# Mixers whose transposed input is split block by block, loads issued from another queue, and transposes moved into products: one change to a thirteen-stage fp32 kernel

## The chip, the cores and the metric

The kernel runs on one core of one Trainium2 chip. The metric is the device time of one execution, in microseconds (us). TensorE is PE in the profile, VectorE is DVE, ScalarE is ACT, GpSimd is POOL, SyncE is SP. A few more names of the profile: PSUM banks hold PE's results (128 partitions x 512 fp32), SBUF holds everything else.

## The reference

Two blocks of two layers each run over x, 256 tokens by 1024 features, batch 1, all in fp32. The thirteen stages in order are ffn, hgrn, ffn, ffn, fox, ffn, ffn, conv, ffn, kv, ffn, nsa, ffn. Cut to what is needed here:

```python
def rmsnorm(x, g): return x * rsqrt(mean(x * x) + EPS) * g
def swiglu(h, w_in, w_out):                 # every ffn stage: x += 0.5 * swiglu(rmsnorm(x))
    gate, up = split(h @ w_in, 2)           # w_in 1024 x 5632
    return (silu(gate) * up) @ w_out        # w_out 2816 x 1024
# hgrn: q, z, i, g = h @ w_in (1024 x 4096); gated linear recurrence; rmsnorm(o) * silu(g) @ w_out
# fox:  q, k, v, g, z_f = h @ w_in (1024 x 4112); attention with forgetting; (o * sigmoid(g)) @ w_out
# conv: b, c, v = h @ w_in (1024 x 3072); causal convolution of width 3 over c * v; (b * y) @ w_out
# kv:   rmsnorm(h, kv_norm) @ w_kv (1024 x 1536); two of its six parts are compressed by a small
#       MLP (w1, gelu, w2) over windows of 32 tokens with position vectors added; it is not added to x
# nsa:  q, gates = h @ w_q; three attentions over the results of kv (compressed, selected, window),
#       with a table of relative biases; mixed by sigmoid gates; @ w_o
```

## The kernel before, in words

**Numbers in two parts.** Every fp32 operand of a large product is split into a high part, rounded to PE's shorter fp32r form, and a low part, the rest. A product is three matmuls per piece k of 128 of the contraction: high times high and the two mixed ones (`pe_product`; lines 385 to 387 feature-major, 128x256, lines 390 to 392 token-major, 128x512). The 256 tokens are two tiles t of 128; the 1024 features are eight pieces k (KT). A feature-major result spans both tiles, so its product needs both tiles' operands from the first matmul on; a token-major one needs one tile.

**Who does what.** SP streams the weights (`raw_in`, `raw_out`). ACT writes each high part (`w_hi`, line 404), DVE each low part (`w_lo`, line 414), and PE multiplies. Products are chunks of 512 columns, numbered through the whole program; while PE is in chunk n, ACT and DVE split chunk n+1. Results alternate between two banks, `bank[0]` and `bank[1]`; four more, `accs`, accumulate over a stage; two, `tr`, take transposes. Each engine's order is fixed by the order of the Python code. Semaphores carry every wait. There is no scheduler.

**Slots.** Within a chunk's product, PE calls a slot function before piece k of tile t; in chunks with slots ACT and DVE call their own slot function in the same place between the parts of their splits (`elementwise_chunk`, by_tile). The slots hold the small work of the mixers: the recurrence's steps in hgrn (`hg_slots`), scores and values in fox (`fx_slots`), the relative biases in ffn 5, the compression in ffn 6 (`pe_compress_slot`, `act_compress_slot`). (ffn 5 and ffn 6 are the sixth and seventh ffn counted from 0, ahead of and behind kv.)

**A stage's start.** x is kept token-major (`x_tok`) and must be transposed and normed. In the mixers PE multiplies x by `diag_`, the identity scaled by 1/rms of each token, so one matmul turns and norms a block (`pe_turn_x`, line 473). The norm is a chain over ACT (squares, line 483; root, line 490) and DVE (lines 521, 523, then `diag_`, line 532). DVE then multiplies by the gain into `xt_full` (line 542), ACT copies the high part (line 510), and DVE subtracts for `xt_lo_` (line 550), each in halves of 128x512 per tile. PE's second tile waits until `xt_full` of the first has been made, and for its own `diag_`, which DVE makes behind the first tile's two scalings:

```python
if s in DIAG: norm(0)
for t in range(NT):
    ...                       # two halves of xt_full
    if s in DIAG and t == 0: norm(1)
    ...                       # two halves of xt_lo_
```

In an ffn the plain x is transposed, and 1/rms is applied to the product's result.

**A mixer's end.** hgrn and fox gate their result `o` (in the arena, a scratch area that the stages share), transpose it in eight blocks per tile (`pe_turn_o`, line 567), split it (`act_turn_o`, `dve_turn_o`, line 585) and multiply by the output weights (`pe_out`). All of it stands behind the last chunk of the input product. In fox that last chunk uses one bank, `bank[0]`, for both tiles, since fox's slots need the other.

**POOL and the loads.** POOL clears `hg_scores` (`pool_hgrn`, line 863) once the stage ahead of hgrn has written x. For kv, ACT issues six loads at the start of ffn 5 (`act_kv_loads`, lines 1444 to 1449): the bias table, a table of one-hot rows (`onehot`), and the compression weights. POOL clears parts of the same arena in `pool_kv`. PE's first bias matmul (line 1507) needs the two tables and POOL's first memset. At slot 18 of ffn 6 ACT also issues eight loads of shifted bias rows (line 1646). In ffn 6 the norm's chain of kv is computed once more, since x is the same.

## Time and profile before

| | us |
|---|---|
| runs of the kernel, in order | 2190.09, 2188.0, 2180.07 |
| median | 2188.0 |
| the profiled execution's own time | 2184.44 |
| its span in the trace | 2183.1 |
| PE busy | 2106.7 (97% of the span) |
| DVE busy | 1202.3 (55%) |
| ACT busy | 1012.9 (46%) |
| POOL busy | 68.2 (3%) |

The mean clock granted to PE over the span is 0.991 of full speed. The span is the time from the first to the last recorded instruction; the execution's own time has 1.3 us around it. Busy times of PE come from modelled ends of matmuls that overlap: in a stream, two 512-column matmuls start 0.23 us apart though each is shown as 0.39. So PE's idle time has to be read from the timeline, where a row's bracket names how long the engine was idle before it and who released it.

### The profile page before, as it was taken

To read this page: it belongs to the slowest core of one execution; us is meant where nothing else is said; L and a number is where in the kernel's file an instruction comes from. 1 tells how busy PE (TensorE), PEld (TensorE's weight loads), DVE (VectorE), ACT (ScalarE), POOL (GpSimd) and SP (SyncE) were. 2 spreads that over 40 slices of the span, in tenths; PEclk is the share of its full clock that TensorE was granted. 3 is DMA by queue.
4 is the path that set the end of the run, shared out by engine and by line. 5 is a ranking of instruction groups with operands and counts; after the bars stand their busy time and mean duration, and the time that the engine had idled before them with its cause. 6 is when DMAs were issued, how large, how long until landed. Compare 5 with 4: busy or idle time off the path is not lost.

```text
span 2183.1 us, 25880 instructions
## 1 busy us (share of the span) xinstructions
PE 2106.7 (97%) x10461; PEld 1754.4 (80%) x10461; DVE 1202.3 (55%) x1456; ACT 1012.9 (46%) x1275; POOL 68.2 (3%) x100
## 2 busy tenths in 40 slices
PE   8998999999999999999999999999999999998999
PEld 6887987888888776788888879878877887787887
DVE  5445687554645564555465556564455455765454
ACT  6344436444544454453354443353446344764342
POOL 1000000000000000000000000070000000000000
PEclk9999999999999999999999999999999999989999
DMA  7553425665555351355555544675636755214553
GB/s 258 194 178 116 155 97 179 196 201 194 196 174 189 130 164 57 131 197 195 192 174 174 196 151 155 192 223 195 174 122 162 218 174 167 88 39 138 190 174 116
DMA packets 265379, 361.02 MB, mean 165 GB/s; under 512 B 19855, under 2 KB 206651, under 8 KB 265132
## 3 DMA queue, kind: packets, MB, share of 16 engines
q1 hardware_dynamic: 256800, 351.57, 49.4%
q10 hardware_dynamic: 7772, 7.17, 1.7%
q8 instruction: 83, 1.36, 0.3%
q0 software_dynamic: 688, 0.62, 0.1%
q14 instruction: 36, 0.29, 0.0%
HBM read 357.75 MB, written 1.57 MB: 165 GB/s over the span
## 4 chain that ended last, share of the span: by engine, by line
PE 89%; DVE 6%; ACT 3%; DMA 1%; issue 1%; ACTq 1%; SPq 0%; POOL 0%; DVEq 0%
PE bank L390 18%; PE bank L392 17%; PE bank L391 17%; PE acc L650 6%; PE acc L652 6%; PE acc L651 6%; PE bank L385 2%; PE bank L386 2%; PE bank L387 2%; PE tr L630 2%; PE acc L680 1%; PE acc L682 1%; PE acc L681 1%; DMA raw_in<-ffn_w_in 1%; DVE w_lo_ L414 1%
## 5 line engine op out<-in xcount | busy, mean ns | idle before, releaser
L390 PE MATMUL bank<-w_hi_,xt_hi_ 128*128 128x512 f32 x1760 | 706.5, 401 | 12.2 <-DVE h_tok L755 5.2
L414 DVE TENSOR_TENSOR w_lo_<-raw_in,w_hi_ 128x2048 fp32r<-128x2048 f32 (+1 forms) x327 | 575.4, 1768 | 236.5 <-ACT w_hi_ L404 236.2
L392 PE MATMUL bank<-w_hi_,xt_lo_ 128*128 128x512 f32 x1760 | 688.7, 391 | 0.0
L391 PE MATMUL bank<-w_lo_,xt_hi_ 128*128 128x512 f32 x1760 | 687.5, 391 | 0.0
L404 ACT ACTIVATE w_hi_<-raw_in 128x2048 fp32r<-128x2048 f32 (+1 forms) x327 | 480.2, 1484 | 81.8 <-PE bank L392 20.9
L760 DVE TENSOR_TENSOR wo_lo_<-raw_out,wo_hi_ 128x2048 fp32r<-128x2048 f32 x80 | 183.9, 2298 | 475.2 <-ACT wo_hi_ L726 475.0
L390 PEld LDWEIGHTS bank<-w_hi_,xt_hi_ 128*128 128x128 f32 x1760 | 332.2, 189 | 79.3 <-issue 6.1
L392 PEld LDWEIGHTS bank<-w_hi_,xt_lo_ 128*128 128x128 f32 x1760 | 331.2, 188 | 71.2
L391 PEld LDWEIGHTS bank<-w_lo_,xt_hi_ 128*128 128x128 f32 x1760 | 332.3, 189 | 62.4
L726 ACT ACTIVATE wo_hi_<-raw_out 128x2048 fp32r<-128x2048 f32 x80 | 153.3, 1916 | 364.5 <-PE acc L652 364.5
L650 PE MATMUL acc<-wo_hi_,ht_hi_ 128*128 128x512 f32 x576 | 224.3, 389 | 1.4 <-DVE ht_lo_ L747 1.3
L651 PE MATMUL acc<-wo_lo_,ht_hi_ 128*128 128x512 f32 x576 | 224.2, 389 | 0.0
L652 PE MATMUL acc<-wo_hi_,ht_lo_ 128*128 128x512 f32 x576 | 224.1, 389 | 0.0
L720 ACT ACTIVATE silu_<-bank,rstd_ 128x256 f32<-128x256 f32 x176 | 83.0, 471 | 220.0 <-PE bank L392 219.8
L650 PEld LDWEIGHTS acc<-wo_hi_,ht_hi_ 128*128 128x128 f32 x576 | 108.1, 188 | 24.6 <-DVE ht_lo_ L747 1.8
L652 PEld LDWEIGHTS acc<-wo_hi_,ht_lo_ 128*128 128x128 f32 x576 | 108.1, 188 | 22.5
L651 PEld LDWEIGHTS acc<-wo_lo_,ht_hi_ 128*128 128x128 f32 x576 | 108.1, 188 | 22.4
L755 DVE SCALAR_TENSOR_TENSOR h_tok<-bank,rstd_,silu_ 128x256 f32<-128x256 f32 x176 | 84.4, 479 | 71.2 <-ACT silu_ L720 71.1
L713 ACT ACTIVATE ht_hi_<-tr 128x512 fp32r<-128x512 f32 x80 | 47.9, 599 | 156.2 <-PE tr L630 156.2
L385 PE MATMUL bank<-xt_hi_,w_hi_ 128*128 128x256 f32 x352 | 99.9, 284 | 4.4 <-DVE xt_lo_ L550 4.4
L386 PE MATMUL bank<-xt_lo_,w_hi_ 128*128 128x256 f32 x352 | 99.6, 283 | 0.0
L387 PE MATMUL bank<-xt_hi_,w_lo_ 128*128 128x256 f32 x352 | 99.6, 283 | 0.0
(322 smaller groups left out, 1866.9 us busy)
## 6 DMA issues: line engine op xcount, KB each, us to landing
raw_in<-ffn_w_in SPq DMA_DIRECT2D x352, 512.0 KB, 4.9
raw_out<-ffn_w_out SPq DMA_DIRECT2D x88, 1024.0 KB, 4.9
raw_in<-hg_w_in SPq DMA_DIRECT2D x16, 1024.0 KB, 5.2
raw_in<-fox_w_in SPq DMA_DIRECT2D x16, 1024.0 KB, 5.5
raw_in<-conv_w_in SPq DMA_DIRECT2D x12, 1024.0 KB, 5.1
raw_in<-hg_w_out SPq DMA_DIRECT2D x4, 1024.0 KB, 5.0
raw_in<-fox_w_out SPq DMA_DIRECT2D x4, 1024.0 KB, 5.0
raw_in<-conv_w_out SPq DMA_DIRECT2D x4, 1024.0 KB, 5.1
```

The lines of the kernel that those rows point to most:

```text
L385: mm(o, wh[:, par, k, c], g.xt_hi_[:, k, :], start=first, stop=False)
L386: mm(o, wh[:, par, k, c], g.xt_lo_[:, k, :], start=False, stop=False)
L390: mm(o, g.xt_hi_[:, k, tok], wh[:, par, k, 0:w], start=first, stop=False)
L391: mm(o, g.xt_hi_[:, k, tok], wl[:, par, k, 0:w], start=False, stop=False)
L392: last = mm(o, g.xt_lo_[:, k, tok], wh[:, par, k, 0:w], start=False, stop=end)
L404: act.e.activation(g.piece(g.wh, n, half, k), raw, ACT.Copy).then_inc(g.w_hi, 4 if k is None else 1)
L414: dve.e.tensor_tensor(g.piece(g.wl, n, half, k), raw, g.piece(g.wh, n, half, k).bitcast(F32), ALU.subtract).then_inc(g.w_lo, 4 if k is Non ...
L650: mm(o, g.hth[:, at, :], g.oh[:, i, cols], start=(c == 0 and i == 0), stop=False)
L651: mm(o, g.hth[:, at, :], g.ol[:, i, cols], start=False, stop=False)
L652: ins = mm(o, g.htl[:, at, :], g.oh[:, i, cols], start=False, stop=False)
L726: act.e.activation(g.oh[:], g.raw_out[:], ACT.Copy).then_inc(g.wo_hi, 2)
L760: dve.e.tensor_tensor(g.ol[:], g.raw_out[:], g.oh[:].bitcast(F32), ALU.subtract).then_inc(g.wo_lo, 2)
```

## The change

Five parts:

1. **Mixer starts.** In hgrn, fox, conv, kv and nsa both tiles' norms and `diag_` come first. PE turns tile 0 into the two `tr` banks and tile 1 into `accs[0]` and `accs[1]`, piece k into bank k%2 of its pair, and the second tile no longer waits for scaling. ACT writes each `xt_hi_` block of 128x128 from PSUM with the gain as its scale, and DVE each `xt_lo_` block from the same bank by one operation (multiply by the gain, subtract the high part); `xt_full` isn't used there. The order is piece by piece over both tiles in hgrn, conv and kv (`BY_K`), tile by tile in fox and nsa. PE waits for the single piece, not a half. The semaphores `xt_hi` and `xt_lo` count 16 per use.
2. **hgrn and fox ends.** The transposes of `o` stand in slots: tile 0 in slots 12 and 14 of the last input chunk, tile 1 in slots 1 and 4 of the first output product, the gating of the blocks spread accordingly. Fox's last chunk uses `bank[1]` for tile 1, and its first sigmoids move to slot 36.
3. **The memset of `hg_scores`** loses its wait and stands at the start of the program on POOL.
4. **The six loads for kv** are issued by POOL, ahead of its memsets in `pool_kv`, and the eight loads of bias rows by POOL in `pool_cmp_bias`.
5. **ffn 6** uses kv's norm. Its tile 0 is turned in slots 2 and 5 of kv's last product, its tile 1 in slots 1 and 2 of its own first. `kv_turn(3)` goes from slot 4 to 6, the gelu from slot 18 to 16. In chunks with slots, the split of the output weights comes behind the slots of the first tile.

The diff, cut (the same edit in further places is left out):

```diff
@@ -71,6 +77,24 @@
     return f * NCH + c + (f >= 3) + (f >= 7)
 
 
+def turn_order(s):
+
+    if s in BY_K:
+        return [(t, k) for k in range(KT) for t in range(NT)]
+    return [(t, k) for t in range(NT) for k in range(KT)]
+
+
+def pieces_for(u, t, k, feature_major, both):
+
+    if both:
+        return 8 * (k // 4) + 8
+    if u in U and U.index(u) in BY_K:
+        return 2 * k + (2 if feature_major else t + 1)
+    if u in U and U.index(u) in DIAG:
+        return 8 * t + k + 1
+    return 8 * t + 4 * (k // 4) + 4
+
@@ -362,12 +386,9 @@
 def pe_product(g, pe, n, t, out, u, w=CW, feature_major=False, slot=None, both=False):
 
 
-    def operands(half):
-        pe.wait_ge(g.w_lo, 8 * n + 4 * half + 4)
-        if both:
-            pe.wait_ge(g.xt_lo, 4 * u + 2 * half + 2)
-        else:
-            pe.wait_ge(g.xt_lo, 4 * u + 2 * (1 if feature_major else t) + half + 1)
+    def operands(k):
+        pe.wait_ge(g.w_lo, 8 * n + 4 * (k // 4) + 4)
+        pe.wait_ge(g.xt_lo, 16 * u + pieces_for(u, t, k, feature_major, both))
 
     wh, wl, par = g.wh, g.wl, n % 2
     tok = slice(t * P, (t + 1) * P)
@@ -377,8 +398,8 @@
         for k in range(KT):
             if slot and k:
                 slot(t * KT + k)
-            if f == 0 and k % 4 == 0:
-                operands(k // 4)
+            if f == 0:
+                operands(k)
             first, end = k == 0, k == KT - 1
             if feature_major:
...
+def turned_piece(g, t, k):
+
+
+    bank = (g.tr[0], g.tr[1], g.accs[0], g.accs[1])[2 * t + k % 2]
+    return bank[:, k // 2 * P:(k // 2 + 1) * P]
+
+
+def pe_turn_half(g, pe, s, t, half):
+    pe_wait_x(g, pe, s, t, half)
+    if s in DIAG:
+        pe.wait_ge(g.diag, 2 * DIAG[s] + t + 1)
+    elif s == 0:
+        pe.wait_ge(g.first_gains, 2)
+    for k in range(4):
+        x = x_tile(g, t, 4 * half + k)
+        if s in DIAG:
+            ins = pe.e.matmul(turned_piece(g, t, 4 * half + k), x, g.diag_[:, t, :], start=True, stop=True)
+        else:
+            ins = pe.e.transpose(turn_bank(g, s, t, half)[:, k * P:(k + 1) * P], x, g.ident[:])
+    ins.then_inc(g.turned, 1)
+
+
...
+def act_mixer_turn_x(g, act, s):
+    act.step(act.e.activation(g.sums[:, 0, 4:5], g.ident[:, 0:1], ACT.Sqrt))
+    for t in range(NT):
+        act_squares(g, act, s, t)
+        act_root(g, act, s, t)
+    act.wait_ge(g.prod, 2 * N0[s])
+    for t, k in turn_order(s):
+        act.wait_ge(g.turned, 4 * turned_before(U[s]) + 2 * t + 2)
+        if k >= 2:
+            act.wait_ge(g.xt_lo, 16 * U[s] + turn_order(s).index((t, k - 2)) + 1)
+        act.e.activation(g.xt_hi_[:, k, t * P:(t + 1) * P], turned_piece(g, t, k), ACT.Copy,
+                         scale=g.gains[:, GAIN[s] + k:GAIN[s] + k + 1]).then_inc(g.xt_hi, 1)
+
+def dve_mixer_turn_x(g, dve, s):
+    for t in range(NT):
+        dve_ms(g, dve, s, t)
+        dve.wait_ge(g.rstd, 2 * R[s] + t + 1)
+        dve.e.tensor_scalar(g.diag_[:, t, :], g.ident[:], g.rstd_[:, t:t + 1], None, ALU.mult).then_inc(g.diag, 1)
+    for i, (t, k) in enumerate(turn_order(s)):
+        dve.wait_ge(g.xt_hi, 16 * U[s] + i + 1)
+        dve.e.scalar_tensor_tensor(g.xt_lo_[:, k, t * P:(t + 1) * P], turned_piece(g, t, k),
+                                   g.gains[:, GAIN[s] + k:GAIN[s] + k + 1],
+                                   g.xt_hi_[:, k, t * P:(t + 1) * P].bitcast(F32), ALU.mult,
+                                   ALU.subtract).then_inc(g.xt_lo, 1)
+
...
+def early_tile(j, turn):
+
+    if j in (KT + 4, KT + 6):
+        turn((j - KT - 4) // 2)
+
+
+def pe_out(g, pe, s, u, n, both=False, free=None, late_tile=None):
+
     for c in range(2):
         for t in range(NT):
             if c:
                 pe.wait_ge(g.x_new, 4 * X[s] + t + 1)
-            pe_product(g, pe, n + c, t, g.bank[t], u, both=both)
+            elif free:
+                free(t)
+            slot = (lambda k: late_tile(k // 4) if k in (1, 4) else None) if late_tile and (c, t) == (0, 0) else None
+            pe_product(g, pe, n + c, t, g.bank[t], u, both=both, slot=slot)
 
...
 def pe_ffn
-    if f == 6:
-        pe.wait_ge(g.hr_done, J_KV + 3)
-    pe_turn_x(g, pe, s)
+    if f != 6:
+        pe_turn_x(g, pe, s)
 
     def turn(c):
         if c == 0 and f == 0:
@@ -638,7 +697,6 @@
             pe.wait_ge(g.kv_vc, 1)
             pe.wait_ge(g.kv_kc, 1)
             pe.wait_ge(g.kv_vcb, 2)
-            pe.wait_ge(g.kv_kct, 4)
         pe.wait_ge(g.ht_lo, 12 * f + c + 1)
         pe.wait_ge(g.wo_lo, 2 * m_of(f, c) + 2)
 def act_ffn
+        def between():
+            if c and slot_c:
+                weights_out()
+            if c:
+                turn(c - 1)
+
...
 def pool_hgrn(g, pool):
-    for i in range(4):
-        pool.wait_ge(g.x_new, 4 * X[S_HGRN - 1] + i + 1)
+
     pool.e.memset(g.hg_scores[:], 0.0).then_inc(g.hg_zero, 1)
...
 def pe_hgrn
+    def beside(c, j):
+        slot((c - 4) * 2 * KT + j)
+        if c == 7:
+            early_tile(j, lambda half: turn_o(0, half))
+
...
             pe_product(g, pe, n0 + c, t, g.bank[t], u, feature_major=c < 4, slot=slot_c if c >= 4 else None)
-    pe_turn_o(g, pe, U_HGRN_O, lambda t, k: g.hg_o[:, k // 4, t, (k % 4) * P:(k % 4 + 1) * P],
-              lambda t: (g.hg_out, 12 + 4 * t))
-    for t in range(NT):
-        pe.wait_ge(g.hg_silu_g, 2 + t + 1)
-    pe_out(g, pe, S_HGRN, U_HGRN_O, n0 + 8)
+    pe_out(g, pe, S_HGRN, U_HGRN_O, n0 + 8, free=lambda t: pe.wait_ge(g.hg_silu_g, 2 + t + 1),
+           late_tile=lambda half: turn_o(1, half))
 
...
 def pe_fox
                 pe.wait_ge(g.fx_v, i)
+            elif i < 7:
+                pe.wait_ge(g.fx_g, i - 4)
             else:
-                pe.wait_ge(g.fx_g, i - 4)
-            pe_product(g, pe, n0 + c, t, g.bank[0], u, slot=slot_c)
-    pe_turn_o(g, pe, U_FOX_O, lambda t, k: g.fx_tmp[:, t, k * P:(k + 1) * P], lambda t: (g.fx_gated, 2 * t + 2))
-    pe.wait_ge(g.fx_g, 4)
-    pe_out(g, pe, S_FOX, U_FOX_O, n0 + 8)
+                pe.wait_ge(g.fx_s, 2 * FOX_HEADS)
+                pe.wait_ge(g.fx_pt, 2 * FOX_HEADS)
+            pe_product(g, pe, n0 + c, t, g.bank[i // 7], u, slot=slot_c)
+    pe_out(g, pe, S_FOX, U_FOX_O, n0 + 8, free=lambda t: pe.wait_ge(g.fx_g, 2 + t + 1),
+           late_tile=lambda half: turn_o(1, half))
 
...
-def act_kv_loads(g, act):
+def pool_kv(g, pool):
     t = g.t
     for i in range(4):
...
-    for i in range(4):
         pool.wait_ge(g.x_new, 4 * X[S_FFN[5] - 1] + i + 1)
+    pool.e.dma_start(g.relb[0:N_BUCKETS], t["rel_bias_2"]).then_inc(g.rel_in, 16)
+    pool.e.dma_start(g.onehot[0:REL_ROWS], t["c_rel"]).then_inc(g.rel_in, 16)
+    pool.e.dma_start(g.w1[0:DH], t["cmp_w1_k_2"].rearrange("(j d) h -> d j h", d=DH)).then_inc(g.compress_in, 16)
+    pool.e.dma_start(g.w1[DH:P], t["cmp_w1_v_2"].rearrange("(j d) h -> d j h", d=DH)).then_inc(g.compress_in, 16)
+    pool.e.dma_start(g.w2[:, 0], t["cmp_w2_k_2"]).then_inc(g.compress_in, 16)
+    pool.e.dma_start(g.w2[:, 1], t["cmp_w2_v_2"]).then_inc(g.compress_in, 16)
...
 def pe_kv, pe_compress_slot
                 pe.wait_ge(g.hr_normed, J_KV + j - 1)
-            slot = lambda k, j=j: pe_hidden(g, pe, 8 * (j - 1) + k % KT)
+            def slot(k, j=j):
+                pe_hidden(g, pe, 8 * (j - 1) + k % KT)
+                if j == 3 and k % KT in (2, 5):
+                    pe_turn_half(g, pe, S_FFN[6], 0, k % KT // 5)
...
-    if j == 4:
-        pe.wait_ge(g.scaled, 4 * S_FFN[6] + 4)
+    if j in (1, 2):
+        pe.wait_ge(g.hr_done, J_KV + 3)
+        pe_turn_half(g, pe, S_FFN[6], 1, j - 1)
+    elif j == 6:
+        pe.wait_ge(g.scaled, 4 * 6 + 4)
```

The order of instructions on DVE at the start of hgrn, before. The last writes of x (line 776), then two norms (lines 521, 523, 532) around the scalings:

```order
L776 SCALAR_TENSOR_TENSOR x_tok<-acc,x_tok 128x512 x4
L521 TENSOR_SCALAR row_sums<-row_sums 128x1
L523 RECIPROCAL rstd_<-row_sums 128x1
L532 TENSOR_SCALAR diag_<-ident,rstd_ 128x128
L542 TENSOR_TENSOR xt_full<-tr,gains 128x512 x2
L521 TENSOR_SCALAR row_sums<-row_sums 128x1
L523 RECIPROCAL rstd_<-row_sums 128x1
L532 TENSOR_SCALAR diag_<-ident,rstd_ 128x128
L550 TENSOR_TENSOR xt_lo_<-xt_full,xt_hi_ 128x4x128 x2
L542 TENSOR_TENSOR xt_full<-tr,gains 128x512 x2
L550 TENSOR_TENSOR xt_lo_<-xt_full,xt_hi_ 128x4x128 x2
L414 TENSOR_TENSOR w_lo_<-raw_in,w_hi_ 128x2048
```

And with the change (line 858 is 776 before; 582, 584 and 591 are the norm; 594 the new operation, of which 16 follow one another):

```order
L858 SCALAR_TENSOR_TENSOR x_tok<-acc,x_tok 128x512 x4
L582 TENSOR_SCALAR row_sums<-row_sums 128x1
L584 RECIPROCAL rstd_<-row_sums 128x1
L591 TENSOR_SCALAR diag_<-ident,rstd_ 128x128
L582 TENSOR_SCALAR row_sums<-row_sums 128x1
L584 RECIPROCAL rstd_<-row_sums 128x1
L591 TENSOR_SCALAR diag_<-ident,rstd_ 128x128
L594 SCALAR_TENSOR_TENSOR xt_lo_<-tr,gains,xt_hi_ 128x128
L594 SCALAR_TENSOR_TENSOR xt_lo_<-acc,gains,xt_hi_ 128x128
L594 SCALAR_TENSOR_TENSOR xt_lo_<-tr,gains,xt_hi_ 128x128
```

Both norms now stand ahead of the first block, and the blocks read `tr` and `accs` (named acc) by turns.

PE at the end of hgrn before: the last matmuls of the input product, the 16 transposes of `o` (line 567) and the output product:

```order
L390 MATMUL bank<-w_hi_,xt_hi_ 128x512
L391 MATMUL bank<-w_lo_,xt_hi_ 128x512
L392 MATMUL bank<-w_hi_,xt_lo_ 128x512
L567 MATMUL tr<-ident,arena 128x128 x16
L390 MATMUL bank<-w_hi_,xt_hi_ 128x512
L391 MATMUL bank<-w_lo_,xt_hi_ 128x512
L392 MATMUL bank<-w_hi_,xt_lo_ 128x512
```

PE in the last chunk of hgrn with the change (lines 411 to 413 are 390 to 392 before, line 620 is 567):

```order
L413 MATMUL bank<-w_hi_,xt_lo_ 128x512
L620 MATMUL tr<-ident,arena 128x128 x4
L411 MATMUL bank<-w_hi_,xt_hi_ 128x512
L412 MATMUL bank<-w_lo_,xt_hi_ 128x512
L413 MATMUL bank<-w_hi_,xt_lo_ 128x512
L411 MATMUL bank<-w_hi_,xt_hi_ 128x512
L412 MATMUL bank<-w_lo_,xt_hi_ 128x512
L413 MATMUL bank<-w_hi_,xt_lo_ 128x512
L620 MATMUL tr<-ident,arena 128x128 x4
L411 MATMUL bank<-w_hi_,xt_hi_ 128x512
```

The first two groups of four transposes stand between products of the input's last chunk; the other two stand likewise in the output product.

ACT's queue at the start of ffn 5 before, from the roots of the norm to the first gate:

```order
L490 ACTIVATE row_sums<-row_sums 128x1 x2
L1444 DMA arena<-rel_bias 32x16
L1445 DMA arena<-c_rel 33x512
L1446 DMA arena<-cmp_w_k 64x32x128
L1447 DMA arena<-cmp_w_v 64x32x128
L1448 DMA arena<-cmp_w_k 128x64
L1449 DMA arena<-cmp_w_v 128x64
L404 ACTIVATE w_hi_<-raw_in 128x512 x4
L720 ACT_TABLE_LOAD
```

POOL's queue with the change, for the same loads (line 867 is a small memset of fox, lines 1587 to 1589 are `pool_kv`'s memsets):

```order
L867 MEMSET arena 128x8x2
L1581 DMA arena<-rel_bias 32x16
L1582 DMA arena<-c_rel 33x512
L1583 DMA arena<-cmp_w_k 64x32x128
L1584 DMA arena<-cmp_w_v 64x32x128
L1585 DMA arena<-cmp_w_k 128x64
L1586 DMA arena<-cmp_w_v 128x64
L1587 MEMSET arena 1x16
L1589 MEMSET arena 128x512
```

On ACT, the split (line 404 before) now follows the roots directly. On POOL the loads stand ahead of the two memsets.

## Rows read from the trace of the kernel before

**Rows 1.** The page, part 1: engine, busy us (share of the span), instructions.

```profile
PE 2106.7 (97%) x10461; PEld 1754.4 (80%) x10461; DVE 1202.3 (55%) x1456; ACT 1012.9 (46%) x1275; POOL 68.2 (3%) x100
```

**Rows 2.** Waits of PE: releaser, us in all, times, longest us.

```profile
PE tr L473 <- DVE diag_ L532: 19.8, 10, 3.8
```

**Rows 3.** Timeline, start of hgrn: start us, us, engine, operation, [idle before <-releaser].

```profile
201.74 2.66 POOL L863 MEMSET arena<- 128x3072 f32 x1 [190.26 <-DVE x_tok L776]
...
202.21 2.26 DVE L532 TENSOR_SCALAR diag_<-ident,rstd_ 128x128 f32<-128x128 f32 x1
...
204.62 3.61 PE L473 MATMUL tr<-diag_,x_tok 128*128 128x128 f32 x16 [3.76 <-DVE diag_ L532]
...
213.51 0.35 PE L385 MATMUL bank<-xt_hi_,w_hi_ 128*128 128x256 f32 x1 [1.47 <-DVE xt_lo_ L550]
...
213.94 0.28 PE L385 MATMUL bank<-xt_hi_,w_hi_ 128*128 128x256 f32 x1
...
214.29 0.28 PE L385 MATMUL bank<-xt_hi_,w_hi_ 128*128 128x256 f32 x1
```

**Rows 4.** Timeline, start of conv.

```profile
1303.15 0.14 DVE L521 TENSOR_SCALAR row_sums<-row_sums 128x1 f32<-128x1 f32 x1
...
1303.33 0.30 ACT L490 ACTIVATE row_sums<-row_sums 128x1 f32<-128x1 f32 x1 [0.56 <-DVE row_sums L521]
...
1304.29 2.02 PE L473 MATMUL tr<-diag_,x_tok 128*128 128x128 f32 x16 [1.78 <-DVE diag_ L532]
...
1304.87 0.18 ACT L483 ACTIVATION_READ_ACCUMULATOR sq_junk<-x_tok 128x1 f32 x1
...
1308.10 2.02 PE L473 MATMUL tr<-diag_,x_tok 128*128 128x128 f32 x16 [1.78 <-DVE diag_ L532]
...
1311.59 0.35 PE L385 MATMUL bank<-xt_hi_,w_hi_ 128*128 128x256 f32 x1 [1.47 <-DVE xt_lo_ L550]
```

**Rows 5.** Timeline, fox: its first product, its second chunk's low half.

```profile
748.31 0.48 PE L390 MATMUL bank<-w_hi_,xt_hi_ 128*128 128x512 f32 x1
...
758.52 2.29 DVE L414 TENSOR_TENSOR w_lo_<-raw_in,w_hi_ 128x2048 fp32r<-128x2048 f32 x1 [1.18 <-ACT w_hi_ L404]
```

**Rows 6.** Groups by line and shape, DVE in hgrn: busy us, mean ns | idle before.

```profile
L1070 DVE SCALAR_TENSOR_TENSOR arena<-acc,small,hg_gain 128x128 f32<-128x128 f32 x16 | 4.5, 344 | 0.0
```

**Rows 7.** Timeline of PE, ends of hgrn and of fox.

```profile
339.11 0.39 PE L392 MATMUL bank<-w_hi_,xt_lo_ 128*128 128x512 f32 x1
...
342.78 0.47 PE L390 MATMUL bank<-w_hi_,xt_hi_ 128*128 128x512 f32 x1
...
895.54 0.50 PE L390 MATMUL bank<-w_hi_,xt_hi_ 128*128 128x512 f32 x1 [1.72 <-ACT arena L1355]
...
903.30 1.25 PE L567 MATMUL tr<-ident,arena 128*128 128x128 f32 x8 [1.15 <-DVE xt_lo_ L585]
```

**Rows 8.** Timeline: a load at the program's start, then the start of ffn 5.

```profile
9.86 0.57 POOL L2144 DMA_DIRECT2D masks<-c_masks  x1
...
1414.02 0.60 PE L1507 MATMUL acc<-arena 33*16 33x512 f32 x1 [0.28 <-DMA arena<-c_rel]
...
1421.41 0.63 ACT L404 ACTIVATE w_hi_<-raw_in 128x512 fp32r<-128x512 f32 x1 [9.37 <-issue]
...
1425.96 0.79 PE L390 MATMUL bank<-w_hi_,xt_hi_ 128*128 128x512 f32 x1 [5.25 <-DVE h_tok L755]
```

**Rows 9.** Windows, PE in ffn 5: window, us, busy (x), clock, DMA share, GB/s.

```profile
1426.00:1429.90 3.90, 3.90 (x9) 0.50 1.04 318
...
1432.00:1435.90 3.90, 3.90 (x21) 1.00 0.89 250
```

**Rows 10.** Timeline of PE, ffn 6: start, first product, compression slots.

```profile
1651.25 0.60 PE L1116 MATMUL tr<-ident,arena 128*128 128x128 f32 x4
...
1657.36 0.78 PE L390 MATMUL bank<-w_hi_,xt_hi_ 128*128 128x512 f32 x1
...
1676.51 0.28 PE L1613 MATMUL acc<-arena 128*15 128x64 f32 x2 [1.34 <-ACT arena L1639]
```

More of the change, by code:

```diff
@@ L544, in dve_turn_x @@
[L544 to L551 removed]
+            dve_scaled(g, dve, s, t, half, gain)
@@ L697, in act_ffn @@
     n0 = N0[s]
-    act_turn_x(g, act, s, first)
+    if f == 6:
+        for half in range(2):
+            act_high(g, act, s, 1, half)
+    else:
+        act_turn_x(g, act, s, first)
     if loads:
@@ L742, in dve_ffn @@
     n0 = N0[s]
-    dve_turn_x(g, dve, s, FFN_GAIN[f], first)
+    if f == 6:
+        for half in range(2):
+            dve_low(g, dve, s, 1, half)
+    else:
+        dve_turn_x(g, dve, s, FFN_GAIN[f], first)
     def turn(c):
@@ L1336, in turn_p, with sigmoids, beside @@
         act.e.activation(g.fx_ptb[:, i % 2, 0:n], g.tr[0][:, 0:n], ACT.Copy).then_inc(g.fx_pt, 1)
-    slot = fx_slots(scores, turn_p, lambda i: None, lambda: None)
+    def sigmoids():
+        act.wait_ge(g.fx_g, 2)
+        for tile in range(NT):
+            first = g.fx_gate[:, tile, 0:CW]
+            act.e.activation(first, first, ACT.Sigmoid).then_inc(g.fx_sig, 1)
+    slot = fx_slots(scores, turn_p, lambda i: None, lambda: None, sigmoids)
+    def beside(c, j):
+        slot((c - 5) * 2 * KT + j)
+        if c == 7:
+            early_tile(j, lambda half: act_turn_o(g, act, U_FOX_O, n0 + 7, 0, half))
     for c in range(4, 8):
@@ L1349, in read @@
                 return
[L1350 to L1355 removed]
+            act.e.activation(cols, g.bank[t][:], ACT.Sigmoid).then_inc(g.fx_g, 1)
         if c == 5:
@@ L1577, in read @@
                 return
+            if j == 3:
+                for half in range(2):
+                    act_high(g, act, S_FFN[6], 0, half)
             if j >= 1:
```

328 lines of the change are left out of this document (168 added, 160 removed).

## The prediction

> **What bounds the kernel.** I read the page first. TensorE (PE) is busy for 2106.7 of 2183.1 us [rows 1]. So the other engines matter only where PE stands still, and the most that any reordering can bring is the idle rest, about 76 us with the start of the program, plus what the clock loses behind the gaps. Next I read who PE waits for: the largest item is the wait for `diag_`, ten waits, two in each of the five mixers, 19.8 us [rows 2]. Then the timeline at each place where PE stops, since a share says nothing on what a stop is worth. Seven places carry the sum.
>
> **Starts of the mixers, before.** I count from the end of the last matmul of the stage ahead, E. Conv is the clean example: the first transposes start 1.78 after E, so E is 1302.51. They take 2.02. The second tile's wait for its own `diag_` starts them at E+5.59, and the first product, whose operand spans both tiles, starts at E+9.08 [rows 4]. A k of that product takes 0.35 (213.94 to 214.29) [rows 3]; the eight ks of its first feature half end at E+11.9. Kv has the same gaps. Hgrn has more: a POOL memset of 2.66 starts at 201.74, and DVE's `diag_`, otherwise 0.29, lies beside it for 2.26; PE then transposes for 3.61 instead of 2.02, and the product starts at 213.51, 12.65 after its E of 200.86 [rows 3]. Its first half ends at E+15.45.
>
> **Starts, after.** Both norms now run ahead of all scaling. The second tile's squares are read out at 1304.87+0.18, E+2.54; from a norm's first operation to PE's transposes it is 1304.29-1303.15 = 1.14 [rows 4]. So the second transposes can start at E+3.83, right behind the first, in their own banks. 1.75 earlier.
>
> The split is then 16 ACT and 16 DVE operations of 128x128 instead of 4 ACT and 8 DVE ones of 128x512. Nothing in the trace before is this operation. The nearest row is a DVE operation of the same kind, shape and PSUM source, 344 ns alone and 4.5 us for 16, so 0.28 each in a series [rows 6]. For ACT I take 0.34 too: one column alone takes 0.30, and a handover between engines 0.04 [rows 4]. Bounds for one piece: 0.28 (a series) below, 0.76 above (0.34+0.34+2 x 0.04, if ACT and DVE take strict turns); no reason allows a gain below 0.28.
>
> - Feature-major (hgrn, conv, kv): four banks are in turn, so DVE's 0.28 sets the pace. The second tile's first piece is in ACT at E+5.9, in DVE from E+6.3; DVE ends the sixteenth at 6.3+14x0.28+0.34 = E+10.6, and the last k ends at E+10.95. Against 11.9 that is 0.95 for conv and for kv; against 15.45 it is 4.5 for hgrn, of which 3.55 is the memset, now issued at the program's start, where DVE has no such operation near.
> - Token-major (fox, nsa): PE needs only four pieces, and could start 1.75 earlier. But two banks are in turn, so a pair costs a round trip of 0.76, 0.38 a piece, and DVE ends at 4.23+15x0.38+0.34 = E+10.3. Before, it ends one operation of 128x512 behind the start of the product, 9.08+0.7 = E+9.8 (0.7, my estimate, is half of the 1.47 for which PE waited for two [rows 4]): 0.5 later. What stands behind it in the queues is late by that. In fox the second chunk's low part ended at 758.52+2.29 = 760.81, and PE, from 748.31 on, came to its second half at about 762.3 [rows 5] (48 matmuls of the first chunk and 12 of the second, 0.23 each); it will ask at 760.5 and get it at 761.5 or so. Fox keeps 0.6 of 1.75. In nsa, ACT starts its narrow split only after a DVE operation behind the turn (the gain's scaling, line 2000) and then has one operation after the other up to the sigmoid that PE waits for already. Nsa loses 0.5.
>
> Starts together: 4.5+0.6+0.95+0.95-0.5 = 6.5.
>
> **Ends of hgrn and fox.** From the last product's final matmul (339.11, +0.23 to the next) to the output product at 342.78 lie 3.4 us [rows 7]. The sixteen transposes move into slots of the last product and of the output product; a group of four costs 0.36 there by the spacing of the matmuls around it, 1.44 in all. Hgrn gains 2.0. Fox has 1.15 of the same wait, its stretch is 3.2, so 1.75. Its last chunk also waited 1.72 for its one bank [rows 7]; now tile 1 has bank 1 and the sigmoids are gone from that point: 1.7. Late next: each output piece goes through DVE, behind gates and splits. The second tile's `xt_lo_` is wanted 5.5 us after the output product starts, and by the durations above is there after 5.0. Together 5.45.
>
> **Ffn 5.** Six loads are issued by ACT; its next split came after 9.37 in which it computed nothing, and PE stood for 5.25 [rows 8]. Behind that gap the granted clock is 0.50 (1.2 instead of 2.4 GHz): 9 matmuls in 3.90 us where 21 pass at 1.00, so 2.2 more are lost [rows 9]. The loads move to POOL, and ACT splits at once. 7.4.
>
> **Ffn 6.** From the heads' transposes at 1651.25 to the first product at 1657.36 are 6.1 us [rows 10]. The first tile is now turned inside kv's last product into idle accumulators, the second inside ffn 6's first; kv's norm serves ffn 6 too, so four squares, two roots and four small DVE operations go. What stays between is one ACT piece and one DVE piece of 512 columns behind kv's last matmul, 1.6 us, and 16 transposes in slots, 1.4. That is 3.1, and 0.6 for product matmuls no longer at half clock: 3.7. In the compression slots the gelu moves two slots up and ACT's eight issues behind it go to POOL; PE's wait of 1.34 goes [rows 10]. The output weights' split, now behind the slots, is hidden by 8 us until its first reader. 1.3.
>
> **Sum.** 6.5+5.45+7.4+3.7+1.3 = 24.4 against the profiled execution's 2184.4 gives 2160. The profiled execution lies 3.6 below the median of the runs (2188.0), which themselves span 10; I keep its base.
>
> **Rivals.**
>
> *POOL's queue is now the late one.* PE's bias matmul at 1414.02 already ended its wait with a load [rows 8]; it also needs a memset that now stands on POOL behind all six loads. A load of 448 KB took POOL 0.57, so six take 3.4 from 1406 and nothing waits. But if this queue stands as ACT's did (9.37 over the six), the memset ends at about 1415.7, and PE's bias matmul comes 2.0 late; at worst the whole term of 7.4 is given back. Middle 4.5, 2164.5. The Trainium skill, "SBUF — State Buffer", section "SBUF: two separate sides", speaks for this: DVE can lock GpSimd out of a shared port, and GpSimd then cannot write the descriptors of its own loads. The memset beside `diag_` shows such a blocking the other way round (2.26 for 0.29 [rows 3]). Chance 0.2.
>
> *Pieces at 0.5 us.* With a pace of p for all pieces, the change gives 47.5-72p in place of 24.4 (42p from three feature-major mixers, 30p from the other two). At 0.5: 11.5, so 2173. For it: every piece waits for another engine. Against: four banks. Chance 0.1.
>
> *Strict turns, slower than before.* At the mixers' starts ACT and DVE do not overlap, 0.76 a piece: 47.5-54.7 = -7.2, so 2191.6. It decides from 0.66 a piece. Against it: nothing but a bank ties the two. Chance 0.03.
>
> *More goes than counted.* The token-major pieces run at 0.28 too (30 x 0.1 = 3.0), fox keeps its whole 1.75 (1.15 more), and ffn 6 saves nearly all of its 6.1 (2.4 more), with 1.4 for clock that comes back behind gaps now gone: 8 more, 2152. Chance 0.15.
>
> **Numbers.** The forecast has 0.5, the rest of 0.02 is unnamed. The likeliest is 2160. The range 2150 to 2173 takes in the POOL rival, the half-speed pieces at their edge and the better case; outside are strict turns and what is unnamed. About 0.5% (11 us) is what a measurement of this kernel can tell from no change, so faster means under 2177: all cases but strict turns and a part of the slow pieces. Faster 0.93, same 0.05, slower 0.02.
>
> **What would show it.** In the profile after: no PE wait over 0.3 at the second tile's transposes; `xt_lo_` pieces 0.28 apart in hgrn, conv and kv; `diag_` at 0.29 in hgrn; the first product of fox 1.75 nearer to E, and a new wait of about 1 in its second chunk; no ACT idle of 9 us and no stretch at 0.50 in ffn 5, with the bias matmul's wait under 0.5; ffn 6's product within 1.6 us of kv's last. A piece over 0.5, a long wait at the bias matmul, or new stretches at 0.50 would make me wrong.

## The result, and the profile after

The changed kernel takes 2164.07 us (median of four runs, 2161.81 to 2167.37) against 2189.05 for the kernel before (four runs, 2180.07 to 2194.18). The ratio is 0.9885, 95% interval 0.9865 to 0.9905: 25 us faster, 21 to 30. The forecast was 2160, a difference of 24.4 to the profiled execution before. The profiled execution shown below is the slowest of the four (2167.37).

The page's head, engine row and clock row of the changed kernel:

```profile
span 2166.1 us, 25994 instructions
...
PE 2109.9 (97%) x10461; PEld 1753.7 (81%) x10461; DVE 1193.7 (55%) x1492; ACT 1021.4 (47%) x1324; POOL 75.0 (3%) x114
...
PEclk9999999999999999999999999999999999889999
```

PE's matmuls are the same in number as in [rows 1], and PE is busy 3 us longer over a span 17 us shorter. So the waits shrank, and some matmuls ran longer: the clock row dips in two slices, before in one. The waits of PE (columns as in [rows 2]):

```profile
PE tr L500 <- DVE diag_ L591: 8.9, 5, 1.8
...
PE bank L411 <- DVE xt_lo_ L535: 3.1, 7, 1.2
PE bank L406 <- DVE xt_lo_ L594: 2.8, 3, 0.9
...
PE acc L708 <- issue: 1.4, 1, 1.4
```

Five of the ten waits for `diag_` are left, all first tiles. The 5.2 for `h_tok` in ffn 5 is gone, and a new wait stands ahead of an output product (line 708, the old 650).

**Where the time went.** The 8632 matmuls of PE that read split weights come in the same order in both kernels. I took the start of each in both traces and followed the difference. It changes at these places (us, the profiled pair; minus is faster; forecast with the prediction's terms). E is the end of the last matmul of the stage ahead.

| place | forecast | measured |
|---|---|---|
| hgrn start | -4.5 | -5.0 |
| hgrn end | -2.0 | -1.3 |
| fox start | -0.6 | -1.2 |
| fox end | -3.45 | -3.5 |
| conv start | -0.95 | -1.45 |
| conv, behind its wait for `xt_lo_` | 0 | +1.6 |
| ffn 5 | -7.4 | -6.0 |
| kv start | -0.95 | -1.5 |
| ffn 6 start | -3.7 | -3.15 |
| ffn 6 compression slots and first output product | -1.3 | -3.35 |
| nsa start | +0.5 | +0.3 |
| rest of nsa | 0 | +5.0 |
| last ffn | 0 | +1.4 |

The places that the change touches bring 26; 8 are given back where it touches nothing. The 1.6, the 1.4 and much of the 5.0 stand in stretches at half clock (windows of PE; window, us, busy, clock, DMA share, GB/s):

```profile
1368.00:1374.00 6.00, 3.71 (x18) 0.83 0.46 168
...
1884.00:1890.00 6.00, 6.00 (x29) 0.50 0.31 122
1890.00:1896.00 6.00, 4.48 (x20) 0.50 0.00 1
1896.00:1902.00 6.00, 5.99 (x27) 0.50 0.00 0
1902.00:1908.00 6.00, 4.49 (x10) 0.51 0.35 91
...
1974.00:1980.00 6.00, 4.70 (x17) 0.72 1.04 360
```

Added up over the program without its first 30 us, both traces hold 41 us at half clock. The change removed those in hgrn, ffn 5 and ffn 6 (13.7 in all); others stood in conv and the last ffn, and nsa had 34 instead of 27. Nsa, from its E to the next stage's transposes, took 137.7 before and 143.0 after. The experiments ask which of this belongs to the change, and which to one execution.

**The steps, seen in the trace.** Conv's start, the counterpart of [rows 4] (timeline; here E is 1292.38):

```profile
1294.16 2.02 PE L500 MATMUL tr<-diag_,x_tok 128*128 128x128 f32 x16 [1.78 <-DVE diag_ L591]
1296.10 2.02 PE L500 MATMUL acc<-diag_,x_tok 128*128 128x128 f32 x16
...
1298.16 0.37 ACT L564 ACTIVATE xt_hi_<-acc,gains 128x128 fp32r<-128x128 f32 x1 [1.57 <-PE acc L500]
...
1298.57 0.35 DVE L594 SCALAR_TENSOR_TENSOR xt_lo_<-acc,gains,xt_hi_ 128x128 fp32r<-128x128 f32 x1 [1.59 <-ACT xt_hi_ L564]
...
1298.83 0.34 DVE L594 SCALAR_TENSOR_TENSOR xt_lo_<-tr,gains,xt_hi_ 128x128 fp32r<-128x128 f32 x1
...
1299.06 0.35 PE L406 MATMUL bank<-xt_hi_,w_hi_ 128*128 128x256 f32 x1 [0.94 <-DVE xt_lo_ L594]
...
1302.19 0.34 DVE L594 SCALAR_TENSOR_TENSOR xt_lo_<-acc,gains,xt_hi_ 128x128 fp32r<-128x128 f32 x1
```

The second tile's transposes follow without a wait. DVE's pieces start 0.26 apart and end at E+10.15 (forecast 0.28, E+10.6). PE starts at E+6.68 and goes at DVE's pace. Fox is bound by the round trip of two banks:

```profile
739.37 0.61 DVE L594 SCALAR_TENSOR_TENSOR xt_lo_<-tr,gains,xt_hi_ 128x128 fp32r<-128x128 f32 x2 [0.67 <-ACT xt_hi_ L564]
740.16 0.61 DVE L594 SCALAR_TENSOR_TENSOR xt_lo_<-tr,gains,xt_hi_ 128x128 fp32r<-128x128 f32 x2 [0.18 <-ACT xt_hi_ L564]
...
753.07 2.29 DVE L435 TENSOR_TENSOR w_lo_<-raw_in,w_hi_ 128x2048 fp32r<-128x2048 f32 x1 [1.19 <-ACT w_hi_ L425]
```

A pair takes 0.79 (forecast 0.76). The second chunk's low part ends at 755.36; PE waited for it 0.08, not 1: it ends 0.4 later than before counted from E, not 0.7, and PE itself came 0.6 later than computed, in part behind a delay of 0.35 at the heads' transposes.

Ffn 5, from POOL's third load to the new wait (the loads, POOL's big memset, PE's bias matmul, ACT's split, PE's output product):

```profile
1397.71 1.15 POOL L1583 DMA_DIRECT2D arena<-cmp_w_k  x1
...
1401.25 0.53 POOL L1589 MEMSET arena<- 128x512 f32 x1
...
1403.93 0.60 PE L1646 MATMUL acc<-arena 33*16 33x512 f32 x1
...
1418.36 1.92 ACT L425 ACTIVATE w_hi_<-raw_in 128x2048 fp32r<-128x2048 f32 x1 [5.40 <-DMA raw_in<-ffn_w_in]
...
1423.44 0.47 PE L708 MATMUL acc<-wo_hi_,ht_hi_ 128*128 128x512 f32 x1 [1.43 <-issue]
```

POOL issued all six loads by 1401.1, and the bias matmul waited for nothing. But ACT now stood idle for 5.40, until a chunk of ordinary weights had landed. `ht_hi`, behind this split in ACT's queue, was late, and PE waited 1.43 for what is made from it.

### The profile page after: what moved, and what is told of

Read it like the earlier page. It is cut to its first block, busy times and chain, and to the rows that moved or that the text cites. A ratio compares the mean times of both kernels' runs of the same rounds, so it can differ in the third digit from the quotient of the medians.

```text
span 2166.1 us, 25994 instructions
## 1 busy us (share of the span) xinstructions
PE 2109.9 (97%) x10461; PEld 1753.7 (81%) x10461; DVE 1193.7 (55%) x1492; ACT 1021.4 (47%) x1324; POOL 75.0 (3%) x114
## 4 chain that ended last, share of the span: by engine, by line
PE 89%; DVE 6%; ACT 3%; issue 1%; DMA 1%; SPq 0%; ACTq 0%; DVEq 0%; POOL 0%
PE bank L411 18%; PE bank L413 17%; PE bank L412 17%; PE acc L708 6%; PE acc L710 6%; PE acc L709 6%; PE bank L406 2%; PE bank L407 2%; PE bank L408 2%; PE tr L689 2%; PE acc L738 1%; PE acc L740 1%; PE acc L739 1%; DVE w_lo_ L435 1%; DVE x_tok L858 1%
```

## The experiments

Twelve runs follow; the first is the changed kernel once more. Times are medians of four to ten executions; each run has one trace. Offsets of two traces at the program's start (up to 1.0) are taken off where a place is given.

**The changed kernel once more.**

> The changed kernel once more, nothing altered. Theory: what the change itself brought is the same at every place (hgrn start 4.9, hgrn end 1.3, fox start 1.2, fox end 3.5, conv start 1.4, ffn 5 6.0, kv start 1.4, ffn 6 6.5), and only the stretches at half clock differ from the first trace (there 1.6 lost behind conv's gap, some 5 in nsa, 1.1 in ffn 7): 2160 to 2167. Rival: those stretches belong to the change and stand at the same places again, 2166 to 2168.

Measured: 2165.33 (2162.6 to 2166.65). At every place that the change touches, save one, the trace equals the first within 0.1. The one is ffn 6's first output product, which came 1.4 later. ACT's split that waits for weights, then PE's product, in the kernel before (lines 404 and 650), the same split in the first trace of the changed kernel, and both in this one:

```profile
1701.50 1.92 ACT L404 ACTIVATE w_hi_<-raw_in 128x2048 fp32r<-128x2048 f32 x1 [5.68 <-DMA raw_in<-ffn_w_in]
1706.47 0.50 PE L650 MATMUL acc<-wo_hi_,ht_hi_ 128*128 128x512 f32 x1 [1.34 <-DVE ht_lo_ L747]
...
1674.70 1.92 ACT L788 ACTIVATE wo_hi_<-raw_out 128x2048 fp32r<-128x2048 f32 x1 [8.41 <-DMA raw_out<-ffn_w_out]
...
1675.42 1.91 ACT L788 ACTIVATE wo_hi_<-raw_out 128x2048 fp32r<-128x2048 f32 x1 [9.77 <-DMA raw_out<-ffn_w_out]
1683.43 0.50 PE L708 MATMUL acc<-wo_hi_,ht_hi_ 128*128 128x512 f32 x1 [1.46 <-DVE ht_lo_ L821]
```

In each, ACT waits for weights to land, and what PE needs is made behind that. In the changed kernel PE waited 0.10 with an idle of 8.41, and 1.46 with one of 9.77. So the first trace's gain of 1.25 at this product isn't a steady part of the change, and ffn 6 as a whole gained 6.5 there and 5.1 here.

Conv's half clock stood again, that in the last ffn did not, and nsa took 140.7 instead of 143.0, again with some 24 us in a row at half clock:

```profile
1884.00:1890.00 6.00, 5.73 (x26) 0.52 0.44 162
1890.00:1896.00 6.00, 4.90 (x22) 0.50 0.00 1
1896.00:1902.00 6.00, 5.58 (x25) 0.50 0.00 0
1902.00:1908.00 6.00, 4.48 (x8) 0.50 0.14 38
```

So the half clock behind single waits of 2.2 comes and goes: the theory holds for it. For nsa neither does. Eight traces of the changed kernel and its variants without filled waits in nsa show it at 139.8 to 143.5, on the mean 141.6; three of the kernel before and its variants (below) at 137.7, 135.5 and 140.3, on the mean 137.8. The two groups overlap, and the 140.3, with 34 us at half clock, is the kernel before with nothing but its loads moved. The granted clocks of all executions, traced or not, show no loss: 0.9888 on the mean of 37 of the kernel before, 0.9911 on the mean of eight of the changed one. With two levels that is some 49 and 38 us at half clock, 10.5 less, and the traces have 13.7 less in hgrn, ffn 5 and ffn 6 and some 3 more in conv and the last ffn. So it isn't shown that the change costs nsa more than the 0.3 at its start. One thing there is new in every trace with the new starts: a wait of 2.0 behind the first product of nsa. In two of the eleven (spread loads, and filled waits in nsa) 6.8 us at half clock followed it and cost 2.3 and 2.0.

**Only the memset moved, in the kernel before.**

```diff
 def pool_hgrn(g, pool):
-    for i in range(4):
-        pool.wait_ge(g.x_new, 4 * X[S_HGRN - 1] + i + 1)
     pool.e.memset(g.hg_scores[:], 0.0).then_inc(g.hg_zero, 1)
```

> The kernel before, with nothing but POOL's memset of hg_scores moved to the start of the program. Theory (the forecast's term): the memset costs hgrn's start 3.55: 1.97 of longer diag_ and 1.59 of PE's transposes at half clock behind the longer wait: about 2185.4 against 2189, and in the trace diag_ at 0.29 and the product at E+9.1. Rival: only the 1.97 is the memset's; PE's slow transposes belong to the wait as such and stay, 2187.

Measured: 2183.66 (ten executions), ratio 0.9975 (0.9965 to 0.9986). In the trace the product starts at E+9.09 (E is 200.31) instead of E+12.65, a gain of 3.6 (forecast 3.55):

```profile
201.66 0.29 DVE L532 TENSOR_SCALAR diag_<-ident,rstd_ 128x128 f32<-128x128 f32 x1
202.10 2.02 PE L473 MATMUL tr<-diag_,x_tok 128*128 128x128 f32 x16 [1.78 <-DVE diag_ L532]
...
209.40 0.36 PE L385 MATMUL bank<-xt_hi_,w_hi_ 128*128 128x256 f32 x1 [1.47 <-DVE xt_lo_ L550]
```

`diag_` is back at 0.29 and the transposes at 2.02. The rival, which left PE's slow transposes in place, falls: the memset costs twice, once on DVE and once in PE's clock behind the longer wait. The interval of the ratio is 3 to 8 us, and holds the 3.6.

**Only the loads moved, in the kernel before.** The edit is the change's own (the six loads and the eight of bias rows), with nothing else of it.

> The kernel before, with only the loads for kv (six, and the eight of bias rows) issued by POOL. Theory: the gain in ffn 5 is this part's alone, 5.25 of the wait and 2.2 of clock, less the new wait of 1.4 that a_late_w1 showed to come from the transfers: 6.0, about 2183. Rival: part of the measured 6.0 came from other parts of the change (the norm, the transposes): 4 or less.

Measured: 2180.08, ratio 0.9953 (0.9937 to 0.9969), 7 to 14 us less. In the trace ffn 5 gains 5.7, and the new wait stands there as well, 1.97 long:

```profile
1433.08 0.47 PE L650 MATMUL acc<-wo_hi_,ht_hi_ 128*128 128x512 f32 x1 [1.97 <-issue]
```

Ffn 6 lost 0.7 behind its start, in a longer stretch at half clock, and gained 1.5 in the compression slots and at the output product. So nearly all of ffn 5's term belongs to the loads' queue, and so does the new wait.

**The compression weights later.** In the changed kernel, all four of their loads, two of 1 MB and two small ones; the lines cut below are those loads, moved here:

```diff
 def pool_positions(g, pool):
+    pool.wait_ge(g.prod, 2 * (N0[S_FFN[5]] + 4))
...
     pool.wait_ge(g.compress_in, 16 * 4)
```

> The changed kernel with the four loads of compression weights issued by POOL only when ffn 5's fourth chunk has been multiplied. Theory: the wait of 1.43 in ffn 5 (ACT's split waited 5.4 for its weights, whose loads were under way beside these) is contention of transfers; it goes, 1.5 us faster (2162.5). Rival: SP's issue of the weights was late for a reason of its own (its four issues took 5.8): the wait stays and the time with it.

Measured: 2163.41 (2159.26 to 2164.98), ratio 0.9877 (0.9858 to 0.9896). ACT's queue at the place:

```profile
1410.73 1.91 ACT L425 ACTIVATE w_hi_<-raw_in 128x2048 fp32r<-128x2048 f32 x1
1414.43 0.60 ACT L775 ACTIVATE ht_hi_<-tr 128x512 fp32r<-128x512 f32 x1 [1.79 <-PE tr L689]
```

The split follows at once, no 5.40, and PE's wait is gone; its product gains 1.7. Over all traces the wait stands in each of the eight with the early loads, 1.4 to 2.9 long, and in none of the four with late ones. The cause of the new wait is shown: the compression weights, 2 MB nearly all in two loads, under way beside the streamed ones. The median is 0.7 to 1.9 lower than the two of the changed kernel, within their scatter.

**The transposes of `o` behind the last chunk again.**

```diff
 def early_tile(j, turn):
-    if j in (KT + 4, KT + 6):
-        turn((j - KT - 4) // 2)
+    return
```

and all four groups ahead of the output product on PE, ACT and DVE.

> The changed kernel with the 32 transposes of o in hgrn and fox put back behind the last input chunk; fox keeps its second bank and early sigmoids. Theory: the trace put 1.3 of hgrn's and 1.7 of fox's gain on this, so about 3 us slower (2167), with waits of 1.0 to 1.4 for xt_lo back at both places. Rival: the transposes cost as much in slots as behind them (each group delays the products by 0.4 to 0.8) and the gates are what counted: no difference within 1.

Measured: 2167.67, 3.0 above the middle of the two medians of the changed kernel. Both waits are back:

```profile
336.55 1.25 PE L620 MATMUL tr<-ident,arena 128*128 128x128 f32 x8 [1.39 <-DVE xt_lo_ L635]
...
895.18 1.25 PE L620 MATMUL tr<-ident,arena 128*128 128x128 f32 x8 [1.15 <-DVE xt_lo_ L635]
```

The difference to the changed kernel's trace is 1.3 in hgrn and 1.5 in fox. The theory stands, and the rival falls.

**All mixers tile by tile.** `BY_K = ()`, and a feature-major product waits for the second tile's piece.

> The changed kernel with all five mixers split tile by tile, none piece by piece. Theory: a feature-major product needs both tiles, so the first product of hgrn, conv and kv starts only behind the tenth piece, about 1.6 later, and two banks in turn make a pair a round trip: 1 to 2 us lost in each of three mixers, 3 to 6 in all (2168). Rival: DVE's 0.26 a piece stays the pace and PE catches up, since the last piece sets the end: under 1 in all.

Measured: 2165.98 (2162.39 to 2168.38): by the medians neither. The trace decides: hgrn is later by 1.5, conv by 1.4, kv by 1.4. PE's wait ahead of the first product is 1.87 (0.94 with pieces in turn), and behind it, in all three, the clock falls, as it doesn't in the changed kernel (windows of conv and kv; in hgrn it falls at 209.6):

```profile
1302.00:1308.00 6.00, 6.00 (x40) 0.73 0.01 3
1596.00:1602.00 6.00, 6.00 (x42) 0.77 0.01 3
```

Conv's later half clock was absent in this trace, which hides 1.6 of the 4.3 from the total. A single trace per kernel can't say that the clock always falls there.

**The output weights' split ahead of the slots again.** `weights_out()` ahead of the chunk in ffn 5 and 6.

> The changed kernel with the splits of the output weights in ffn 5 and ffn 6 put back ahead of the chunk with slots. Theory: this order is what took the wait of 1.3 ahead of ffn 6's first output product (the low half of h was late there); it comes back, 1.2 slower, 2166. Rival: what is late there is the load of the output weights beside POOL's loads; then ACT now waits for it ahead of the slots and 3 or more are lost.

Measured: 2167.49 (2162.62 to 2168.6), 2.8 above the same middle, with executions that overlap those of the changed kernel. The split of the output weights and the product:

```profile
1678.08 1.92 ACT L788 ACTIVATE wo_hi_<-raw_out 128x2048 fp32r<-128x2048 f32 x1 [10.20 <-DMA raw_out<-ffn_w_out]
1686.08 0.50 PE L708 MATMUL acc<-wo_hi_,ht_hi_ 128*128 128x512 f32 x1 [1.92 <-DVE ht_lo_ L819]
```

A wait of 1.92 stands ahead of the product, but the order of the splits is not what makes it. ACT's idle for the landing of the output weights and PE's wait go together in every trace in which POOL issues the loads and the bias rows aren't spread: 8.41 and 0.10, 8.47 and 0.15, 8.64 and 0.30, 8.64 and 0.33, 9.29 and 0.96, 9.77 and 1.46, 10.42 and 2.10 with the new order, 9.19 and 0.88, 10.20 and 1.92 with the old one. PE's wait is the idle less 8.3 each time. So the theory falls for this wait: it is as long as the weights are late. The rival had that cause, but not the place, since ACT's idle is behind the slots. What the old order does cost is seen in the slots: a wait of 0.8, with 0.5 left of it ahead of the product. In all this trace loses 3.9 in ffn 6, 1.6 of it in a stretch at half clock behind the wait.

**Filled waits in nsa.** Idle transposes of the identity into free banks:

```diff
+def fill(g, pe, bank, n):
+    for i in range(n):
+        pe.e.transpose(bank[:, i % 4 * P:(i % 4 + 1) * P], g.ident[:], g.ident[:])
     def values(h):
+        if h in (4, 9):
+            pe.wait_ge(g.ns_ql, 8 if h == 4 else 14)
+            fill(g, pe, g.tr[1], 12)
     def c_values(half, banks):
+        if half == 0:
+            fill(g, pe, g.bank[0], 8)
```

> The changed kernel with idle matmuls (transposes of the identity into banks that are free) in three waits of PE in nsa: 12 each ahead of the values of heads 4 and 9, 8 ahead of the compressed values. They compute nothing that is read. Theory: the half clock of nsa, some 24 us in each trace so far, follows a wait of 1.9 in which PE does nothing; with the wait filled the clock stays at full and 4 to 8 us go, 2158 to 2161. Rival 1: the clock falls on what PE does ahead of the wait (many narrow matmuls), so filling changes nothing. Rival 2: DVE and ACT bound this stretch, so the clock comes back and the time doesn't; the fill then costs its overhang, 0.5 to 1.

Measured: 2166.7, nothing gained. Two windows of the changed kernel at 0.50 are at full clock here, and the stretch up to the compressed values gained 4.9. But the second filling took 3.4 of it back:

```profile
1922.27 1.11 PE L1900 MATMUL tr<-ident 128*128 128x128 f32 x4 [4.33 <-DVE ht_hi_ L2186]
```

My wait for the bank of the second filling was for something that DVE makes later than PE needs it: 4.33 instead of 2.20. This trace also lost 2.5 in ffn 5, where the wait for late weights was 2.51 with half clock behind it, and 2.0 at nsa's start. The 24 us in a row that the expectation counts were not in every trace either: with the transposes of `o` put back it was 13.7, and with late compression weights it began not behind the wait of 1.92 but behind one of 2.37. So the result says nothing against the filling, and nothing for it.

**Filled waits in conv and the last ffn.** 14 transposes ahead of conv's output product, 12 in the last ffn between the tiles.

> The changed kernel with 14 idle transposes ahead of conv's output product and 12 behind the first tile's transposes of the last ffn, where PE waits 2.3 and 2.2. Theory: the half clock behind them (1.6 and 1.1 lost in the first trace, present in two and three of the four traces) is gone: 1 to 2 us faster on the median and a narrower spread of the runs. Rival: the clock falls elsewhere instead, or the fill delays the products: no change.

Measured: 2164.67, no change by the median. In the trace (2169.3, the longest span of all variants) both places stay at full clock. Stretches at half clock stood in ffn 5 and ffn 6 behind waits of 2.91 and 2.10, both for late weights, and in nsa. The expectation has the last ffn's stretch in three of the first traces; it stood in the first alone, and in no other of this study, so there was little to win there. Inconclusive alone.

**Loads spread.** In the changed kernel, one of the 1 MB loads behind chunk 3 and one behind chunk 4 of ffn 5, and in `pool_cmp_bias`:

```diff
     for p in range(0, P, COPIES):
+        pool.wait_ge(g.prod, 2 * (N0[S_FFN[6]] + 3 + p // (2 * COPIES)))
...
```

> The changed kernel with POOL's large loads spread: the compression weights one behind ffn 5's third chunk and one behind its fourth, the eight of bias rows in pairs behind chunks 3 to 6 of ffn 6. Theory: both new waits, 1.4 to 2 in ffn 5 and 0 to 2 with some clock in ffn 6 (it stood in three of the traces of the changed kernel, behind an ACT idle of 8 to 10 for the output weights), are the same contention; both go, 2 to 4 faster than the changed kernel on the median: 2161. Rival: only ffn 5's was; then it equals the kernel with late compression weights, 2163.4.

Measured: 2162.03 (2158.41 to 2163.21), ratio 0.9875 (0.9852 to 0.9898). Neither wait stands in the trace, and ACT's idle of 8 to 10 ahead of the output weights in ffn 6 is 5.1, ended by PE and not by a load. With the compression weights alone issued late it was still 8.64, so here it is the spread bias rows that count, in this trace and in the two that follow: ffn 6's wait has the same kind of cause as ffn 5's. By the medians 2 to 3 faster than the changed kernel.

**Spread and filled.**

> The same, and in nsa 12 idle transposes ahead of the values of head 4 and 8 ahead of the compressed values (not those ahead of head 9's, whose bank was still being read, so that PE waited 4.3 there). Theory: in the trace of the first filling the stretch from head 4 to the compressed values took 4.9 less; that stays now, and nothing is lost behind it: 3 to 5 faster than without: 2157. Rival: DVE bounds the stretch up to the end of the stage, and the gain is taken back there: within 1 of the kernel without the filling.

Measured: 2157.2 (2155.47 to 2158.14), ratio 0.9857 (0.9839 to 0.9875), 4.8 faster than without the filling; the executions of the two do not overlap, by 0.3. Windows over the same stretch, spread alone:

```profile
1884.00:1890.00 6.00, 6.00 (x28) 0.50 0.23 91
1890.00:1896.00 6.00, 4.47 (x21) 0.50 0.00 1
1896.00:1902.00 6.00, 5.86 (x26) 0.50 0.00 0
```

spread and filled:

```profile
1884.00:1890.00 6.00, 2.44 (x21) 1.00 0.01 1
1890.00:1896.00 6.00, 6.00 (x28) 0.52 0.00 0
1896.00:1902.00 6.00, 5.98 (x35) 0.91 0.31 94
```

Half clock in nsa falls from 41 us to 14, and nsa from 143.0 to 136.7. Of this, 6.8 us of half clock and 2.3 us of time stood at nsa's start, ahead of the first filled wait, where the two kernels don't differ; the filling's share is 20 and 4.0. Half clock moved behind another wait (of 2.37, for DVE), which is not filled.

**And the two other fillings.**

> The last kernel, spread loads and filled waits in nsa, with the 14 idle transposes ahead of conv's output product and the 12 at the start of the last ffn as well. Theory: behind these two waits the clock stays at full; the trace of the last kernel loses 1.4 behind conv's wait and about 1 behind the other, but not every execution does: 1 to 2 faster, 2155.5. Rival: the median doesn't move, as when these two alone were added to the changed kernel (2164.7 beside 2164.1): 2157.

Measured: 2155.54 (2153.34 to 2158.31), ratio 0.984 (0.9817 to 0.9862): the fastest kernel of this study, 35 us under the kernel before (30 to 40 by the interval) and 8.5 under the changed one's median. Against the last kernel the medians differ by 1.7 with overlapping executions, as far as the theory went, but not settled: conv's place gained 1.2 in the trace, the last ffn had no half clock to lose in either, and the rest came in nsa, where this edit changes nothing. Conv's window:

```profile
1368.00:1374.00 6.00, 5.13 (x36) 1.00 0.44 162
```

## Why the prediction was right, and where not

**The starts (6.5, measured 8.9).** All steps went the predicted way, most of them a little better: the pace was 0.26, not 0.28, DVE's last piece ended 0.45 earlier than computed, and a feature-major start brought 1.4 to 1.5, not 0.95. The memset's term was right (3.6 against 3.55). The two-bank pace was right (0.39 against 0.38), and so was nsa's small loss. The wait of 1 in fox did not come (0.08). What was tested by itself is the memset and the order of the pieces; the split in blocks and the two norms ahead were not undone, and their terms are read from the traces.

**The ends of hgrn and fox (5.45, measured 4.8).** Fox came as computed, with 1.9 at the bank and 1.6 at the transposes instead of 1.7 and 1.75. The step "a group of four costs 0.36" failed in both: a group costs 0.44, since the product matmul behind it is slower too, and in hgrn the first cost 0.8, with a wait of 0.17 for the gate.

**Ffn 5 (7.4, measured 6.0).** The removal was right. What was late next was missed: I asked who waits for POOL's queue, not what the six transfers do to the weights once they no longer wait for ACT. Undone, it is worth 1.7.

The rival *POOL's queue is the late one* fell: 4.4 for the six issues instead of 3.4, and no wait at the bias matmul. The Trainium skill ("SBUF — State Buffer", "SBUF: two separate sides") tells of DVE, in operations of a 2-port mode, locking GpSimd out of the shared port. The trace of ffn 5 shows no such block: the longest issue took 1.15 us. It doesn't say whether the DVE operations beside the loads were of that mode. That POOL's memset holds up DVE's `diag_`, the other direction, is shown by the second experiment.

**Ffn 6 (5.0, measured 6.5 and 5.1).** The start was over-valued by 0.55: 1.8 stayed between the products instead of 1.6, and the groups of transposes cost more than 0.36. In the slots I counted one wait of three. That of 0.73 went as well, in both executions of the changed kernel. That of 1.34 ahead of the output product went in the first and stood at 1.46 in the second; it depends on when the output weights land, which no step of the prediction looked at. That the term came out at 5.1 is therefore luck in part: an over-valued start, one wait more, and a third that comes and goes. The new start of ffn 6 was not undone by itself.

**The sum.** 24.4 forecast, 26 found at the places, 17.0 by the two spans, 25 by the medians. The spans differ from the medians since the profiled execution before lies 4.6 under its median and the one after 3.3 above. Taking the profiled execution as the base explains the 4 us between 2160 and 2164. That 25 comes so near to 24.4 is luck in part: the starts brought 2.4 more and ffn 5 1.4 less, hgrn's end 0.7 less, and half clock that comes and goes is worth several us in either median. The sign of error "new stretches at 0.50" did come, in conv and the last ffn; it shows that the prediction counted half clock only where a wait went, never where a wait stayed. *Pieces at 0.5* and *strict turns* fell with 0.26. *More goes than counted* did not come: the token-major pieces ran at 0.39, fox kept 1.2 of its 1.87, and ffn 6's start brought less, not more. Each of six ffn starts is also 0.1 later (PE waits 0.34 for `xt_lo` instead of 0.22), 0.7 in all; no run tells why.
